# First layer's head of a hybrid encoder: x loaded first, modulation in four pieces, gate chunks inside the next pair

## The reference

```
shift, scale, gate = split(silu(c) @ mod_w + mod_b, 3)      # c: one row for the prompt, 8 for the samples
hmod = rms_norm(x, norm_pre) * (1 + scale) + shift
u    = hmod @ w_in                  # x_a (512), g_a (512), q, k, v, g_b (512)
x_a  -> causal conv of width 4 -> RG-LRU recurrence -> times silu(g_a)
q, k, v -> rope, sliding-window attention with sinks -> times silu(g_b)
x    = x + gate * rms_norm(concat(y_a, y_b) @ w_out, norm_post)
```

## Time and profile before

| | us |
|---|---|
| median of three runs | 1355.41 (1355.38 to 1356.03) |
| span of the profiled execution | 1354.8 |
| TensorE busy in the span | 1325.8 (98%) |
| VectorE, ScalarE, GpSimd busy | 855.6, 434.6, 331.1 |

### The profile page before, as it was taken

One profiled execution on the slowest core, in us unless ns is written; L12 is line 12 of the kernel. 1 busy time (PEld: TensorE's weight loads), 2 busy tenths in 40 slices (PEclk: granted clock), 3 DMA queues, 4 the chain that ended last, 5 costly groups with the idle time before them and its releaser, 6 DMA issues.

```text
span 1354.8 us, 27409 instructions
## 1 busy us (share of the span) xinstructions
PE 1325.8 (98%) x11200; PEld 904.0 (67%) x11200; DVE 855.6 (63%) x1939; ACT 434.6 (32%) x1044; POOL 331.1 (24%) x450
## 2 busy tenths in 40 slices
PE   5999999999999999999999999999999999999997
PEld 3577776666654454667877788877788777875543
DVE  3847874355454375785886858858578586782246
ACT  3213443344431233521422414224143241432221
POOL 1023200010013232523312423224222242212352
PEclk9999999999999999999999999999999999999999
DMA  9531016002034522121212112121121211440124
GB/s 356 235 75 36 5 36 271 8 1 79 3 130 167 195 85 108 13 81 19 71 46 68 34 34 83 38 77 40 34 83 29 75 50 34 127 159 26 35 94 168
DMA packets 63297, 111.96 MB, mean 83 GB/s; under 512 B 34778, under 2 KB 38690, under 8 KB 61618
## 3 DMA queue, kind: packets, MB, share of 16 engines
q1 hardware_dynamic: 63172, 110.21, 24.2%
HBM read 91.79 MB, written 18.40 MB: 81 GB/s over the span
## 4 chain that ended last, share of the span: by engine, by line
PE 88%; DVE 7%; POOL 1%; DMA 1%; issue 1%; ACT 1%; SPq 0%; DVEq 0%; POOLq 0%; ACTq 0%
PE psum L1132 83%; PE psum L1135 5%; DVE mem L2963 1%; DVE mem L2774 1%; DVE mem L3288 1%; DMA mem<-x_dram 1%; DVE mem L3054 0%; DMA y<-mem 0%; DVE mem L3165 0%; DVE mem L2943 0%; DMA mem<-x 0%; POOL mem L954 0%; DVE mem L2780 0%; ACT mem L1915 0%; ACT mem L2087 0%
## 5 line engine op out<-in xcount | busy, mean ns | idle before, releaser
L1132 PE MATMUL psum<-mem 32*32 32x32 f32 (+12 forms) x10592 | 1264.1, 304 | 4.9 <-DVE mem L2475 1.5
L1132 PEld LDWEIGHTS psum<-mem 128*128 128x128 f32 (+4 forms) x10592 | 835.7, 143 | 401.7 <-issue 217.0
L2963 DVE SCALAR_TENSOR_TENSOR mem<-mem 128x576 f32<-128x576 f32 (+1 forms) x126 | 106.1, 842 | 0.0
L1135 PE MATMUL psum<-mem 128*128 128x128 f32 (+1 forms) x608 | 85.1, 278 | 17.2 <-ACT mem L1927 12.9
L1135 PEld LDWEIGHTS psum<-mem 128*128 128x128 f32 (+1 forms) x608 | 70.7, 144 | 41.4 <-issue 21.0
L2278 ACT ACTIVATE mem<-mem 128x128 f32<-128x128 f32 x72 | 22.0, 305 | 127.6 <-DVE mem L3213 74.4
L2164 ACT ACTIVATE mem<-psum 128x288 f32<-128x288 f32 x28 | 11.4, 407 | 104.0 <-PE psum L1132 104.0
L1011 POOL COPY mem<-mem 128x3 f32<-128x3 f32 x24 | 8.4, 348 | 148.9 <-DVE mem L2921 70.1
L2056 ACT ACTIVATE mem<-mem 128x256 f32<-128x256 f32 x72 | 35.5, 495 | 26.4 <-DVE mem L2697 26.4
L2744 DVE TENSOR_TENSOR mem<-mem,psum 128x512 f32<-128x512 f32 x28 | 19.1, 684 | 37.4 <-PE psum L1132 37.0
L2174 ACT ACTIVATE mem<-mem 128x576 f32<-128x576 f32 (+1 forms) x42 | 32.7, 779 | 28.0 <-DVE mem L2941 28.0
(11 more groups left out here) (260 smaller groups left out, 1277.2 us busy)
## 6 DMA issues: line engine op xcount, KB each, us to landing
mem<-modw SPq DMA_DIRECT2D x12, 2048.0 KB, 12.2
mem<-w SPq DMA_DIRECT2D x44, 512.0 KB, 4.3
mem<-x SPq DMA_DIRECT2D x10, 512.0 KB, 4.7
x_dram<-mem SPq DMA_DIRECT2D x9, 512.0 KB, 2.9
mem<-row_dram SPq DMA_DIRECT2D x8, 576.0 KB, 5.2
mem<-x_dram SPq DMA_DIRECT2D x9, 512.0 KB, 3.7
mem<-wout SPq DMA_DIRECT2D x1, 4096.0 KB, 15.0
mem<-gs SPq DMA_DIRECT2D x8, 512.0 KB, 3.6
```

What stands on the lines that cost most here:

```text
L1132: return pe.matmul(*a, **k)
L1135: return pe.transpose(out, in_, ident[0:n, 0:n])
L2963: x = dve.scalar_tensor_tensor(cvm, U1[:, m, lo + j:hi + j], CW[:, 3 * g + ORDER[m], j:j + 1], cvm, ALU.mult, ALU.add)
```

## The change

- SP issues the first group of x before the three constants, and all of x before any modulation weights.
- The shift and scale come in four pieces (`PIECES`) of two row blocks each: 256 columns of the shift and 256 of the scale in one slot, by two DMAs of 1 MB with runs of 1 KB. One product, one bias addition, one set of 4 transposes and one set of reductions serve both.
- All nine tiles of x are transposed first, through banks 6 and 7 (a half of a tile each), with a semaphore for each half.
- The projections `xa` follow piece by piece: two row blocks, both columns, one third of the tokens.
- The two gate chunks are computed inside pair 0, after step "1", the row products after steps "6" and "2". `mod_done` now counts both multiplies.
- T1 is made by GpSimd; VectorE makes T2, T3, T4 in this order. The loads of the pair's weights wait for 3 instead of 6 chunks. Two semaphores are merged into others (`gate_ev` into `mod_done`, `kc_in` into `wqkv_in`).

```
-MOD_ORDER = (0, 2, 1, 3, 4, 5)
-MOD_SLOT = (0, 1, 2, 0, 1, 2)
+PIECES = KT // 2
+PIECE_W = 2 * P
+PIECE_SLOT = (0, 1, 2, 0)
+GATE_SLOT = (1, 0)
+FIRST_DIFF = {"t1": 1, "t2": 2, "t3": 3, "t4": 4}
+H_MOD = {(q, n): 7 * q + (0, 2, 5)[n] for q in range(PIECES) for n in range(3)}
+H_ALL = 7 * PIECES
...
 # SP
+            def mod_piece(q):
+                slot = PIECE_SLOT[q]
+                if q >= 3:
+                    sp.wait_ge(sem("mod_mm"), q - 2)
+                cols = slice(q % 2 * PIECE_W, q % 2 * PIECE_W + PIECE_W)
+                for w in range(2):
+                    sp.dma_start(mw[0][slot][:, :, w * PIECE_W:w * PIECE_W + PIECE_W], I["modw"][0, 2 * w + q // 2][:, :, cols]
+                                 ).then_inc(sem(f"mw_in{slot}"), 16)
+            def mod_gates(i):
+                sp.wait_ge(sem("mod_mm"), (2, PIECES)[i])
+                sp.dma_start(mw[0][GATE_SLOT[i]], I["modw"][0, 4 + i]).then_inc(sem(f"mw_in{GATE_SLOT[i]}"), 16)
...
             piece(0)
+            for ap, name in ((ident, "ident"), (cT, "cT"), (npre, "npre")):
+                sp.dma_start(ap, I[name]).then_inc(sem("const_in"), 16)
             piece(1)
-            mod_first(0)
             mod_rows(0)
-            mod_first(1)
+            piece(2)
+            piece(3)
+            mod_piece(0)
             first_weights(0)
             first_weights(1)
-            piece(2)
-            piece(3)
-            mod_first(2)
-            mod_first(3)
+            mod_piece(1)
+            mod_piece(2)
+            mod_piece(3)
             gate_rows(0)
-            mod_first(4)
-            mod_first(5)
...
+            sp.wait_ge(sem("mod_mm"), 3)
+            pair_weights(0, wB)
+            mod_gates(0)
+            mod_gates(1)
             sp.wait_ge(sem("mod_mm"), 6)
-            pair_weights(0, wB)
             pair_weights(1, wC)
             sp.wait_ge(sem("xa_mm"), 6)
             pair_weights(2, wA)
-            sp.wait_ge(sem("mod_done"), 1)
+            sp.wait_ge(sem("mod_done"), 2)
...
 # GpSimd, after the roots of the norms
+            wait(pool, sem("h_mod"), H_MOD[1, 2] + 3)
+            pool.tensor_tensor(T1, HT[:, 0:HALF, LO:], HT[:, 0:HALF, 0:LO], ALU.subtract
+                               ).then_inc(sem("t_ready"), 1)
...
 # TensorE
+            def turn_x(t):
+                pe.wait_ge(sem("n_xh"), t + 1)
+                for half in range(2):
+                    if t:
+                        pe.wait_ge(sem("n_ev" if half else "n_low"), t)
+                    for j in range(HALF):
+                        k = HALF * half + j
+                        i = tr(B(6 + half)[:, j * P:(j + 1) * P], xh[:, t % 2, k * P:(k + 1) * P])
+                    i.then_inc(sem("n_tp" if half else "n_tp0"), 1)
...
+            for t in range(NT):
+                turn_x(t)
             pe.wait_ge(sem("dve_step"), DVE_STEP["sc_ready"])
-            first_chunk(0, 0)
...
-            gate_turn(0, 1, 6)
+            mod_piece(0, 2)
+            turn_piece(0, 5)
+            for q in range(2):
+                pe.wait_ge(sem(f"w0_in{q}"), 16)
+            xa(0, 0)
+            xa(0, 1)
             pe.wait_ge(sem("n_ev"), NT)
+            mod_piece(1, 6)
+            xa(0, 2, (0,))
+            turn_piece(1, 7)
+            xa(0, 2, (1,))
+            xa(1, 0)
+            mod_piece(2, 6)
+            xa(1, 1)
+            turn_piece(2, 7)
+            xa(1, 2)
+            mod_piece(3, 6)
+            xa(2, 0)
+            turn_piece(3, 7)
+            xa(2, 1)
+            xa(2, 2)
+            for c in range(2):
+                for n in range(3):
+                    xa(3, n, (c,))
+            def gate_part(i):
+                if i == 0:
+                    pe.wait_ge(sem("mod_ev"), PIECES)
+                    pe.wait_ge(sem("h_mod"), H_ALL)
+                    for n in range(2):
+                        mod_chunk(0, 4 + n, GATE_SLOT[n], (3, 5)[n], 6 + n)
+                elif i == 1:
+                    pe.wait_ge(sem("mod_ev"), 6)
+                    gate_turn(0, 0, 6)
+                else:
+                    pe.wait_ge(sem("mod_done"), 1)
+                    gate_turn(0, 1, 6)
...
 # VectorE
-            for t in range(3):
+            for t in range(NT):
                 raw(t)
             dve.wait_ge(sem("modb_in"), 16)
-            mod_chunk(0, 0, 0)
...
+            for q in range(PIECES):
+                piece_rows(q, 6 if q else 2)
+                piece_columns(q, 7 if q else 5)
+                for n in range(3):
+                    modulate(q, n)
...
+            dve.wait_ge(sem("h_mod"), H_ALL)
+            dve.wait_ge(sem("t_ready"), 1)
+            dve.tensor_tensor(T2, halves(1, 1), T1, ALU.subtract).then_inc(sem("t_ready"), 1)
             dve.tensor_tensor(T3, halves(1, 1), halves(0, 1), ALU.subtract).then_inc(sem("t_ready"), 1)
+            dve.wait_ge(sem("t_ready"), FIRST_DIFF["t2"])
+            dve.tensor_tensor(T4, halves(1, 0), T2, ALU.subtract).then_inc(sem("t_ready"), 1)
             mod_chunk(0, 4, 6)
             mod_chunk(0, 5, 7)
+            mod_gate(0, 0, 6, "mod_done")
             mod_gate(0, 1, 6, "mod_done")
```

More of the change, by code:

```diff
@@ L862, in out_diff @@
                 if after:
-                    wait(pool, sem("t_ready"), 4 + OUT_DIFF[after])
+                    wait(pool, sem("t_ready"), T_FIRST + OUT_DIFF[after])
                 for k in range(HALF):
@@ L1139, in mod_chunk @@
                 pe.wait_ge(sem(f"mw_in{slot}"), 16 * load)
-                if l and n >= 2:
+                if n >= 2 and l:
                     pe.wait_ge(sem("mod_ev"), 6 * l - 1 + n)
@@ L1145, in mod_chunk, with mod_piece, turn_piece @@
                 i.then_inc(sem("mod_mm"), 1)
-            def first_chunk(i, bank):
-                mod_chunk(0, MOD_ORDER[i], MOD_SLOT[i], 1 + i // 3, bank)
-            def turn_part(q, bank):
+            def mod_piece(q, bank):
+                slot = PIECE_SLOT[q]
+                pe.wait_ge(sem(f"mw_in{slot}"), 32 * (1 + q // 3))
+                if q:
+                    pe.wait_ge(sem("mod_ev"), q)
+                for k in range(KT):
+                    r = slice(32 * (k % 4), 32 * (k % 4) + 32)
+                    i = mm(B(bank)[r], scT[:, k], mw[0][slot][:, k], start=(k < 4), stop=(k >= 4))
+                i.then_inc(sem("mod_mm"), 1)
+            def turn_piece(q, bank):
+                pe.wait_ge(sem("mod_ev"), q + 1)
+                if q:
+                    pe.wait_ge(sem("h_mod"), H_MOD[q - 1, 0] + 1)
                 for j in range(4):
-                    i = tr(B(bank)[:, j * P:(j + 1) * P], modrow[:, (4 * q + j) * P:(4 * q + j + 1) * P])
+                    at = (j // 2) * D + (2 * q + j % 2) * P
+                    i = tr(B(bank)[:, j * P:(j + 1) * P], modrow[:, at:at + P])
                 i.then_inc(sem("mod_tr"), 1)
+            def turn_x(t):
[7 more added lines that the diff above has]
+                    i.then_inc(sem("n_tp" if half else "n_tp0"), 1)
             def mod_turn():
@@ L1181, in _ @@
             pe.wait_ge(sem("const_in"), 48)
[L1182 to L1192, removed]
@@ L1208, in _ @@
[L1208 to L1218, removed]
-            pe.wait_ge(sem("n_ev"), NT)
[L1220 to L1231, removed]
-            gate_turn(0, 1, 6)
+            def xa(q, n, cs=(0, 1)):
+                for c in cs:
+                    for k in (2 * q, 2 * q + 1):
+                        pe.wait_ge(sem("h_mod"), H_MOD[q, n] + k % 2 + 1)
+                        i = mm(B(c * 3 + n)[:, 0:NC], w0[:, c, k], HT[:, k, n * NC:(n + 1) * NC],
+                               start=(k == 0), stop=(k == KT - 1))
+                    if q == PIECES - 1:
+                        i.then_inc(sem("xa_mm"), 1)
```

132 lines of the change are left out of this document (48 added, 84 removed).

## The result

The changed kernel takes 1370.72 us (median of 4 runs, 1368.77 to 1371.34) against 1355.54 of the kernel before (4 runs): ratio 1.0109, 95% interval 1.0094 to 1.0123. It is 15.2 us slower. The forecast was 1356.9 us, with 1360.0 as the upper end of its range, so it was wrong: the sign of its 1.5 us was right, the size was not.

A forecast was written before the change was run, and what follows sets the result against it. TensorE, busy 98% of the span, was taken as the bound. Profiled span 1354.8, plus 1.5 (1.4 before the first pair, 0.1 for the chain behind the gates) and 0.6 around the span, gave 1356.9 us, range 1353.4 to 1360.0.

The forecast's parts named there:

- part 2: Four-piece modulation and its projections: 43.0 us of TensorE work and waits after the tile stage, with VectorE's work hidden.
- The yardstick: TensorE's start of the first pair, less gate work in front: 78.02 - 7.1 = 70.9 us in the kernel before.
- S: The moment TensorE starts the first pair, without gate work: forecast 72.3 us after the change against 70.9 before.
- Tile stage: Head, scaling and transposing all nine x tiles, paced by ScalarE at 2.1 us a tile: last transposes end at 28.1.
- 43.0 of work and waits: TensorE from last x transposes to the pair: chunks 7.5, piece transposes 2.0, projections 31.0, waits 2.3; sum given as 43.0.
- Slow clock at the first projections: Half-rate TensorE clock during the first chunk and matmuls after x: none to 2.65 us, 1.2 taken.
- First square: ScalarE's first square of x, with x loaded first: starts at about 5.5 us instead of 6.86.
- Loads in 1 KB runs: Loads of the 2 MB modulation pieces: no wait taken; as a rival, slow runs cost 2.9 us more, 1359.8, chance 0.06.
- Gates in the pair: 7.1 us of gate work moved inside the first pair: multiply done 20.0 after S, pair ends 34.3 after; 0.1 charged.
- the clock falls in the tile stage: Rival: first chunk and matmuls after the x transposes all run at 1.2 GHz, 3.5 us slower, 1359.0, chance 0.16.
- it stays up: Rival: TensorE at 2.4 GHz from the third x tile on, 0.5 us faster, 1354.9, chance 0.22.
- the recurrence chain: Rival: GpSimd and VectorE, or eight small loads, take 1 to 3 us longer in the pair, 1358 to 1360, chance 0.08.

The follow-up runs named there:

- gates-alone version: The kernel before, with only its two gate chunks and row products moved into pair 0 and two slots' loads adjusted: 1355.81 us, ratio 0.9998.
- filled version: The changed kernel with T1 on VectorE, GpSimd silent until the last multiply-add, and unread identity transposes in TensorE's tile-stage and first-piece gaps: 1359.4 us, ratio 1.0027.
- T1 twice: The changed kernel, with GpSimd making T1 two times in a row: 1372.74 us, ratio 1.0129 to the kernel before.
- both: The changed kernel, with T1 back on VectorE and GpSimd silent until the last multiply-add: 1360.87 us, ratio 1.0043 to the kernel before.

## Why the prediction was wrong

**The step that failed** is in part 2: VectorE's work for a piece "is an estimated 5 us against 10 us of TensorE, so it hides", and "T1 goes to GpSimd, which is idle, some 20 us before its first reader". GpSimd was idle, and T1's reader was far away; both were true and neither was the question. T1 takes 5.18 us and holds one of VectorE's operations until it ends (5236 ns for 0.41), and the four sums, which the earlier load of the weights also brought forward, hold four or so more by about 1 us each (1.48 and 1.37 for 0.42, 1.67 for 0.73). From the multiply-adds of piece 2 to the bias addition of piece 3 VectorE needed 11.7 us (55.11 to 66.79); the same operations of the last piece took 3.2 (69.30 to 72.48). That is more than the cover, TensorE waited 5.86 where the sum had 0, and the clock took 2.5 more.

The trace of before had shown this where I didn't look, at 71 to 77 us. VectorE's T4, then GpSimd's last two sums, all three on memory:

```profile
71.20 1.22 DVE L2414 TENSOR_TENSOR mem<-psum,mem 128x1024 f32<-128x1024 f32 x1 [3.89 <-PE psum L1132]
72.34 3.12 DVE L2514 TENSOR_TENSOR mem<-mem 128x2304 f32<-128x2304 f32 x1
```
```profile
71.77 1.27 POOL L823 TENSOR_TENSOR mem<-mem 128x512 f32<-128x512 f32 x1
73.12 3.46 POOL L827 TENSOR_TENSOR mem<-mem 128x512 f32<-128x512 f32 x1
```
T4 takes 2.55 elsewhere, the sum 1.27. T4 is issued while the sum of 71.77 runs and begins when it ends at 73.04 (72.34 + 3.12 - 73.04 = 2.42, about its own time); the next sum is issued at 73.12, stands until T4 ends at 75.46, and is done 1.12 later. A row twice as long as its neighbours of the same form points to a resource that the page has no column for. The Trainium skill, "SBUF — State Buffer", section "Who interferes with whom", states the rule: VectorE and GpSimd share one port pair, which is held for a whole instruction by whoever issues first. By that section VectorE's operations with two inputs in memory contend for it, and its tensor_scalar can, in a mode that takes both ports. The runs agree: 0.18 became 4.77 beside T1, while a multiply with one input in PSUM isn't held (L2414 at 71.20, beside the sums of 70.43 and 71.77, took 1.22, and 1.23 alone). This speaks against the change and should have been a rival: 5.2 of T1 and 4 x 1.3 of sums are an estimated 10.4 us of delay against a cover of 5, about 5 us of wait.

**The yardstick.** "Before: 70.9" came from one execution. Its own time I took as 1354.8 + 0.6 = the median, but the executions after the prediction show 2.1 to 2.2 us around the span of the kernel before (1.8 to 1.9 for the change), and so about 1353.3 for a typical span of before. The profiled one was about 1.5 us slower than the median, and its clock had fallen at 26 us, which it did not in the three later profiles of this order. That the clock is what makes executions of before slow fits 15 of the later ones (11 at a mean clock of 0.999 with spans of 1352.3 to 1353.8, four at 0.998 with 1354.2 to 1356.2), but in the other 27 the two groups overlap (1352.3 to 1354.8 at 0.999, 1353.3 to 1356.4 at 0.997 and 0.998), so it is not shown in general. A typical S is 69.1, from the gates-alone version, whose time is that of before. By S the filled version, 72.3, is then 3.2 slower, where I had 1.4.

**The other steps**, with S of after 83.5 against 72.3:
- Tile stage, 28.1 forecast: 29.72. ScalarE scaled the last tile at 27.5 instead of 26.0; 0.3 of it lie in the first square and 1.1 in the wait for the second group of x, which lands at another time in every execution. With x first and the tile stage unchanged it ended at 27.97 to 29.80 in the other profiles without fillers.
- 43.0 of work and waits: 43.6 in the filled version (28.74 to 72.3). Right.
- Slow clock at the first projections, 1.2 forecast: 1.7 in this execution (10.43 against 8.74), none there in three others.
- The wait and the clock behind it, 0 forecast: 5.86 + 2.5. With the 1.6, 0.6 and 0.5 by which the three items above exceed the forecast this is 11.1 of the 11.2 between 83.5 and the forecast S of 72.3. That the filled version also has an S of 72.3 is luck: it has 0.6 more in the tile stage and 0.6 more behind it, and none of the 1.2 forecast for the slow clock.
- First square, 5.5 forecast: 5.79. This came out nearly right by two errors that cancel. The 4.75 from issue to square was one slow load; the first tile lands 3.3 to 3.7 us after its issue in the profiles with x first. And the constants, of whose 1.4 us I took none, cost 1.2, because the tanh waits for them. The gain of 1.07 didn't last past the second square: 10.26 against 10.09.
- Loads in 1 KB runs, no wait forecast: none. They ran at 347 to 349 GB/s from 26 to 42 us, which is nearer to the 374 of the earlier trace rows than to the 221.
- Gates in the pair: the multiply is done 20.1 after S (forecast 20.0), xc is ready at 34.4 (34.1), the gate matmuls are first evicted at 35.5, which with the 0.74 of before between the pair's end and that eviction puts the pair's end at 34.7 (34.3). Right, and alone it costs nothing (1355.81).

**The rivals.** That the clock falls in the tile stage was true as well, for 1.7 us; that it stays up was not, though it did in the profile of "T1 twice" until the wait. The Trainium skill's rule, cited there, fits in part only: the clock did not fall at each of the nine bursts. The 1 KB runs and the recurrence chain cost nothing to be seen. None of them was the cause. By the differences to before, the 15.2 us are 9.7 from GpSimd beside VectorE with the clock it costs (after less "both"), 1.9 from the slow clock of the half-idle tile stage ("both" less the filled version, not clear of the noise), and 3.6 from the rest. I put these 3.6 down to the order itself, since projections that used to fill the wait for ScalarE now start behind it; no version with another order was run that would show it. Of the 3.6, 3.2 are seen at S and 0.4 are not explained. No version tried is faster than the kernel before.

## What to carry to other kernels

Before work is moved to an idle engine, ask what it shares with the busy ones: here a GpSimd operation with both inputs in memory held the next memory operation of VectorE until it ended, even one of 36 elements a lane, so such work belongs where VectorE has nothing that TensorE waits for. Look in the trace for rows that are much longer than their neighbours of the same form; they price a shared resource that no busy share shows. When a load is moved forward, look at what else stands before its first reader: here the reader's engine waited for the constants instead. And compare the profiled execution with the median before its rows become a yardstick: here it was about 1.5 us slow.

## What the runs showed of the hardware

- Beside GpSimd's T1, 5.04 to 5.18 us, one VectorE operation took 4.77 to 5.24 us whatever its size (36 or 384 elements a lane). GpSimd's operations are held in the same way by VectorE's differences (3.46 for 1.27). A VectorE multiply with one input in PSUM was not held (1.22 against 1.23).
- Waits of 3.29 and 5.86 us on TensorE were followed by a granted clock of 0.50 to 0.64, near the 1.2 GHz level, and cost about 3.3 and 2.5 us more. A stage in which it works about half of the time had a fall to 0.57 to 0.62 for a few us, in it or behind it, in five of six profiles without fillers. With unread transposes in the gaps it read 1.00, and 0.999 as the mean of all nine executions. In the first 20 us the column reads 1.00 although the transposes take 424 ns.
- Loads with 1 KB runs moved 347 to 349 GB/s from 26 to 42 us; with long runs, in the kernel before, it was 422 on average from 26 to 47 us.
